# First block of a two-block transformer kernel: input projections on split halves with the low halves made by GpSimd, convolution sums in PSUM, decay logs moved ahead of the convolution's norm

## What is computed

```
h = rms_norm(x);  u = h @ w_in                      # 1024 x 6560
conv, c_q, c_kv, k_rope, hq, hf, hi, hg, u_gate = split(u)
y_a = silu(layer_norm(depthwise_conv31(a * sigmoid(g)) + b)) @ w_conv_out
y_b = attention(rms_norm(c_q) @ w_uq, rms_norm(c_kv) @ w_ukv, k_rope) @ w_attn_out
y_c = hgrn2(hq, hf, hi, hg) @ w_hgrn_out            # recurrence over time with decays
x = x + (sum over branches of sigmoid(u_gate_b) * y_b) @ w_out
x = x + relu(rms_norm(x) @ w_ff1)^2 @ w_ff2
```

## Time and profile before

| | |
|---|---|
| median of three runs | 2350.22 us (2348.99 to 2354.43) |
| the profiled execution, its own time | 2351.7 us |
| its span in the trace | 2349.8 us |
| mean granted TensorE clock | 0.97 of full speed |
| TensorE busy, share of the span | 95% |
| VectorE, ScalarE, GpSimd busy | 63%, 46%, 10% |
| first layer's input stage begins at | 21.0 us |
| second layer's input stage begins at | 609.4 us |

### The profile page before, as it was taken

How to read it: one execution, slowest core, us unless ns; L and a number is a source line. 1 busy time by engine, 2 the same in 40 slices (tenths; PEclk the granted TensorE clock), 3 DMA queues, 4 the chain that set the end, 5 groups by cost and what they waited for, 6 DMA issues and landing times.

```text
span 2349.8 us, 36652 instructions
## 1 busy us (share of the span) xinstructions
PE 2226.4 (95%) x13894; PEld 1878.1 (80%) x13894; DVE 1484.8 (63%) x2286; ACT 1085.5 (46%) x1525; POOL 239.9 (10%) x241
## 2 busy tenths in 40 slices
PE   8999999999999999899999789999999988999997
PEld 6878667999787866799976579887888577888786
DVE  2946355755394635575535577888775357788876
ACT  1142452444114244244433355676654355666665
POOL 1914000101091400011100000000000000000000
PEclk9999899999999989999999889999999998999999
DMA  4432123555343211456533236888865514688884
GB/s 164 144 117 82 63 63 126 175 185 171 125 143 117 81 65 64 144 175 199 185 133 97 74 118 216 306 297 309 296 214 162 161 55 153 227 311 304 304 295 145
DMA packets 109951, 397.38 MB, mean 169 GB/s; under 512 B 12104, under 2 KB 14160, under 8 KB 109520
## 3 DMA queue, kind: packets, MB, share of 16 engines
q1 hardware_dynamic: 108720, 393.98, 49.4%
q10 hardware_dynamic: 1056, 1.06, 0.1%
HBM read 393.93 MB, written 1.06 MB: 168 GB/s over the span
## 4 chain that ended last, share of the span: by engine, by line
PE 81%; DVE 12%; ACT 4%; issue 2%; DMA 1%; SPq 0%; DVEq 0%; ACTq 0%
PE psum L544 79%; DVE W_LO L1689 3%; PE psum L552 1%; DVE region L1694 1%; DMA ring<-in_weights 1%; DVE region L1697 1%; DVE RS L1726 1%; ACT region L1244 1%; ACT W_HI L1239 1%; DVE SQ L1694 1%; ACT SQ L1244 1%; ACT region L1248 0%; DMA PAR<-in_params 0%; ACT L1244 0%; DVE X_LO L1694 0%
## 5 line engine op out<-in xcount | busy, mean ns | idle before, releaser
L1689 DVE TENSOR_TENSOR W_LO<-ring,W_HI 128x1024 fp32r<-128x1024 f32 x435 | 533.0, 1225 | 223.9 <-ACT W_HI L1239 213.7
L1239 ACT ACTIVATE W_HI<-ring 128x1024 fp32r<-128x1024 f32 x435 | 461.8, 1062 | 323.7 <-PE psum L544 240.6
L544 PE MATMUL psum<-HN,ring 128*128 128x272 f32 (+1 forms) x1728 | 416.3, 402 | 9.8 <-DVE HN L1701 9.8
L544 PEld LDWEIGHTS psum<-HN,ring 128*128 128x128 f32 x1728 | 335.6, 196 | 83.1 <-issue 16.7
L544 PE MATMUL psum<-X_HI,W_HI 128*128 128x256 f32 x808 | 231.3, 286 | 8.9 <-DVE W_LO L1689 6.5
L544 PE MATMUL psum<-X_LO,W_HI 128*128 128x256 f32 x808 | 226.9, 281 | 0.0
L544 PE MATMUL psum<-X_HI,W_LO 128*128 128x256 f32 x808 | 226.7, 281 | 0.0
L1248 ACT ACTIVATE region<-psum 128x272 f32<-128x272 f32 (+10 forms) x223 | 89.0, 399 | 278.0 <-PE psum L544 255.6
L1689 DVE TENSOR_TENSOR W_LO<-SQ,W_HI 128x1024 fp32r<-128x1024 f32 x128 | 156.9, 1225 | 36.8 <-ACT W_HI L1239 32.9
L544 PE MATMUL psum<-W_HI,XG_HI 128*128 128x512 f32 x384 | 153.0, 398 | 17.3 <-DVE W_LO L1689 15.3
L544 PE MATMUL psum<-FN_HI,W_HI 128*128 128x272 f32 (+1 forms) x592 | 168.6, 285 | 0.0
(11 more groups left out here) (327 smaller groups left out, 4136.2 us busy)
## 6 DMA issues: line engine op xcount, KB each, us to landing
ring<-in_weights SPq DMA_DIRECT2D x616, 512.0 KB, 4.2
SQ<-in_weights SPq DMA_DIRECT2D x128, 512.0 KB, 4.8
XT<-in_x SPq DMA_DIRECT2D x1, 1088.0 KB, 5.0
CST<-in_consts SPq DMA_DIRECT2D x1, 1082.5 KB, 7.3
SQ<-bias_by_distance ACTq DMA_DIRECT2D x1, 1024.0 KB, 5.3
out<-XT SPq DMA_DIRECT2D x8, 128.0 KB, 1.9
PAR<-in_params SPq DMA_DIRECT2D x1, 572.0 KB, 8.3
bias_by_distance<-MIX ACTq DMA_DIRECT2D x1, 12.0 KB
```

The source lines that it names most:

```text
L544: ins = nc.tensor.matmul(dst, w, x, start=start, stop=stop, skip_group_check=True)
L1239: lane(nc.scalar.activation(W_HI[:, s % SPLIT, :], ring_slot(n), ACT.Copy), split_hi)
L1689: lane(nc.vector.tensor_tensor(W_LO[:, s % SPLIT, :], ring_slot(n), W_HI[:, s % SPLIT, :].bitcast(F32), ALU.subtract), split_lo)
```

## The change

1. The normed input of each layer is also kept as `HN_HI` (ScalarE copies, after the norm) and `HN_LO` (VectorE subtractions). All input chunks but the first two of a layer (`conv_a` 0 and `conv_g` 0) and all 24 gate chunks of a layer become split chunks: 50 in each layer. ScalarE makes their `W_HI`. GpSimd, not VectorE, makes their `W_LO`; it follows only after steps.
2. All four tiles of the convolution are made by VectorE. The running sum lies in PSUM bank 7, held for it; the gated inputs (`glu`) are made between the taps. GpSimd has no taps any more.
3. `hgrn_prep` is taken apart into `hgrn_scaled`, `hgrn_log`, `hgrn_sum` and `hgrn_strip`; the logs now stand ahead of `conv_norm`. ScalarE's Silu of the convolution and its first gate move behind them, and ScalarE's waits get further calls of `follow`. The root of the convolution's variance goes to a tile of its own.
4. The table `bucket` is loaded by a DMA of its own into a buffer used later, which frees room. `mla_q` lets go of its last chunk at its end.

The diff, cut to its core:

```diff
             def conv_in(l):
-                for j in range(4):
-                    project(("conv_a", l, j), hn, ready=None if j else till("normed", KT * 2 * l))
-                    project(("conv_g", l, j), hn)
+                banks.hold(("conv_sum", l), 7)
+                project(("conv_a", l, 0), hn, ready=till("normed", KT * 2 * l))
+                project(("conv_g", l, 0), hn)
+                for j in range(1, 4):
+                    project(("conv_a", l, j), hn_parts, ready=till("hn_split", KT * l) if j == 1 else None, by_pool=True)
+                    project(("conv_g", l, j), hn_parts, by_pool=True)
 ...
             def gate(l, b, m):
                 at = first_column(l)
-                project(("gate", l, b, m), lambda k: HN[:, k, at:], T - at)
+                project(("gate", l, b, m), lambda k: (HN_HI[:, k, at:], HN_LO[k][:, at:]), T - at, by_pool=True)
 ...
+                if r % 2 == 0:
+                    for k in range(KT):
+                        act.wait_ge(sem("normed"), KT * r + k + 1)
+                        fn(HN_HI[:, k, :], HN[:, k, :], ACT.Copy, sem("hn_high"))
 ...
+                else:
+                    for k in range(KT):
+                        dve.wait_ge(sem("hn_high"), KT * (r // 2) + k + 1)
+                        tt(HN_LO[k], HN[:, k, :], HN_HI[:, k, :].bitcast(F32), ALU.subtract, sem("hn_split"))
 ...
+                def taps(j, lo=0, hi=CONV_K):
+                    for i in range(lo, hi):
                         x, w, b = tap(l, j, i)
                         if i == 0:
-                            ts(CO[:, j, :], x, w, b, ALU.mult, ALU.add)
+                            ts(total, x, w, b, ALU.mult, ALU.add)
+                        elif i < CONV_K - 1:
+                            stt(total, x, w, total, ALU.mult, ALU.add)
                         else:
+                            stt(CO[:, j, :], x, w, total, ALU.mult, ALU.add, sem(f"conv_out{j}"))
+                half = CONV_K // 2 + 1
+                glu(0)
+                taps(0, 0, half)
+                glu(1)
+                taps(0, half)
+                glu(2)
+                taps(1, 0, half)
+                glu(3)
+                taps(1, half)
+                taps(2)
+                taps(3)
 ...
+            # on GpSimd
+            def split(s, n):
+                if not splits.by_pool[s]:
+                    return
+                pool.wait_ge(split_hi, s + 1)
+                lane(nc.gpsimd.tensor_tensor(W_LO[:, s % SPLIT, :], ring_slot(n), W_HI[:, s % SPLIT, :].bitcast(F32), ALU.subtract), split_pool)
+            follow = Follower(splits, split)
 ...
             for name, *args in SCHEDULE:
                 if name in steps:
                     steps[name](*args)
+                follow(("step", name, *args))
 ...
-        s += [("conv_in", l), ("conv_taps", l), ("hgrn_in", l), ("mla_in", l), ("hgrn_rows", l), ("conv_norm", l)]
-        s += [("gate", l, 0, 0), ("conv_var", l), ("mla_norm", l), ("hgrn_prep", l)]
+        s += [("conv_in", l), ("conv_taps", l), ("hgrn_in", l), ("mla_in", l), ("hgrn_scaled", l), ("hgrn_rows", l), ("hgrn_log", l)]
+        s += [("conv_norm", l), ("hgrn_sum", l), ("mla_norm", l), ("gate", l, 0, 0), ("conv_var", l), ("hgrn_strip", l), ("conv_silu", l), ("first_gate", l)]
```

More of the change, by code:

```diff
@@ L318, in __init__, with hold @@
         self.psum, self.full, self.free = psum, full, free
-        self.next, self.uses, self.of = 0, [0] * 8, {}
+        self.next, self.uses, self.of, self.held = 0, [0] * 8, {}, set()
+    def hold(self, key, bank):
+        self.of[key] = (bank, self.uses[bank])
+        self.uses[bank] += 1
+        self.held.add(bank)
     def take(self, pe, key, bank=None):
+        while bank is None and self.next in self.held:
+            self.next = (self.next + 1) % 8
         if bank is None:
@@ L462, in build_program @@
         HAT = at_region(3, 4, TP)
+        CONV_ROOT = HAT[:, 0, 0, :T]
+        with ExitStack() as first:
+            sb("unused_first", 4 * KT * T, stack=first)
+            HN_HI, low = (sb(f"HN_{p}", k, T, dtype=F32R, stack=first) for p, k in (("HI", KT), ("LO", KT - 1)))
+            assert (2 * KT - 1) * T <= 16 * 256
+            assert used[0] + T <= size
+            sb("unused_behind", 16 * 256 - (2 * KT - 1) * T + used[0], stack=first)
+            BUCKET = GATES[0][:, 0:2, :].rearrange("p a b -> p (a b)")[:, :384]
+            HN_LO = [low[:, k, :] for k in range(KT - 1)] + [sb("HN_LAST", T, dtype=F32R, stack=first)[:, :]]
         used[0] = work
@@ L558, in columns, with chunk @@
                 return tuple(p[:, lo : lo + n] for p in w) if isinstance(w, tuple) else w[:, lo : lo + n]
-            def chunk(split=False, routed=None):
+            def chunk(split=False, routed=None, by_pool=False):
                 n = state["n"]
@@ L623, in _ @@
             hn = lambda k: HN[:, k, :]
+            hn_parts = lambda k: (HN_HI[:, k, :], HN_LO[k])
             def start():
                 dst, done = take("bucket_bias")
-                mm(dst[:HEADS, :384], PAR[:BUCKETS, PARAMS["rel"][0] : PARAMS["rel"][0] + HEADS], cst("bucket", rows=BUCKETS), done=done)
+                mm(dst[:HEADS, :384], PAR[:BUCKETS, PARAMS["rel"][0] : PARAMS["rel"][0] + HEADS], BUCKET[:BUCKETS, :], done=done)
                 for l in range(DEPTH):
@@ L1338, in conv_norm, with conv_var, conv_silu, ahead @@
                 fn(SQ[:, : 4 * T], CO[:, :, :].rearrange("p k t -> p (k t)"), ACT.Square, sem("conv_squares"))
-                root(("conv_var", l), RS[:, :T], T, 512)
+            def conv_var(l):
+                root(("conv_var", l), CONV_ROOT, T, 512)
+            def conv_silu(l):
+                def ahead(m):
+                    wait_bank("gate", l, 0, m)
+                    follow(("gate", l, 0, m))
+                for m in range(3):
+                    ahead(m)
                 act.wait_ge(sem("conv_scaled"), l + 1)
@@ L1780, in norm, with conv_taps, glu @@
                         split_tile(FN_HI[r // 2][:, k, :], FN_LO[r // 2][:, k, :], HN[:, k, at:], sem("norm_split"))
+                else:
+                    for k in range(KT):
+                        dve.wait_ge(sem("hn_high"), KT * (r // 2) + k + 1)
+                        tt(HN_LO[k], HN[:, k, :], HN_HI[:, k, :].bitcast(F32), ALU.subtract, sem("hn_split"))
                 if r == 2:
                     zeros()
-            def conv_in(l):
-                for j in range(4):
+            def conv_taps(l):
+                bank, uses = banks.of["conv_sum", l]
+                dve.wait_ge(banks.free[bank], uses) if uses else None
+                nc.vector.memset(SM[:, 31:32], 0.0).then_inc(banks.full[bank], 1)
+                dve.wait_ge(banks.full[bank], uses + 1)
+                total = banks.tile(("conv_sum", l))[:, :T]
+                def glu(j):
                     src = wait_bank("conv_a", l, j)
```

93 lines of the change are left out of this document (52 added, 41 removed).

## The result

The changed kernel took **2397.65 us** (median of four runs, 2389.08 to 2400.66) against 2352.32 for the kernel before on the same chip. The ratio is 1.019, with an interval of 1.016 to 1.022: it is slower. I had forecast slower, but 2362 us and at most 2394; the loss is four times what I summed up. Its profiled execution took 2400.66 us (span 2398.9), 49.0 us over that of before.

A forecast was written before the change was run, and what follows sets the result against it. TensorE, busy 95% of the span, was taken to bound the kernel. Terms of +11.7 us in the first layer and -0.6 in the second added +11 to 2351.7, forecasting 2362 us, own range 2339 to 2377, wider range 2326 to 2394.

The forecast's parts named there:

- input stage: Input chunks: split chunks save 18.2 us a layer; the first layer gives back a 5.9 us stand and 2.1 of clock.
- first gates: Eight gates before `branch_out`: split chunks save 5.6 and 5.3 us, less 3 us given back for one late split.
- `branch_out` to first scores: Before the recurrence: GpSimd's splits delay `hgrn_args` 1, 22.7 us to first scores, plus a clock drop of 2.1.
- recurrence: Eight turns, each 2.3 us longer as GpSimd's differences wait behind splits, plus 4 us a layer for two clock drops.
- after it: Gates after the recurrence: split chunks save 5.6 and 5.3 us, less 1.5 for a root delayed by ScalarE's rounding.
- the first half of the pair: Recurrence, from ScalarE's read of gate 2 to turn 3, through rounding, split, differences, clamp and exponential: 12.5 us.
- The stand in the first layer's start: First layer's input stage: TensorE stands 5.9 us for the second `W_LO`, ready at 37.2, then a 2.1 us clock loss.
- 9.5 us a turn: Recurrence: a chain from gate i's end to gate i+2's end, for i = 2, takes 19.0 us for two turns.
- The price of a split: GpSimd's `W_LO` instruction: 1.95 us taken from its 128x1024 differences; the range keeps 2.89, a documentation estimate gave 2.25.
- The rival with the clock: Recurrence: the clock falls in each turn, +12 us in a layer rather than +4, total 2378; chance 0.07.
- stay ahead: Rival: GpSimd finishes splits early, so waits in the recurrence vanish and `branch_out` shrinks; about 2289 us; chance 0.14.
- Disturbed taps: Rival: PSUM sums don't part VectorE and GpSimd; taps 0.66, splits 2.9, `conv_mean` waits; about 2399 us; chance 0.13.

The follow-up runs named there:

- (2): Changed kernel with the eight gate chunks inside the recurrence of each layer plain again, as before the change: 2315.89 us, ratio 0.984.
- (1): Changed kernel with only GpSimd's list reordered, its differences for the next block ahead of its splits: 2338.31 us, ratio 0.991.
- (6): Kernel with plain gates in the recurrence, plus GpSimd's wait for the gate two turns earlier, without split work there: 2373.64 us, ratio 1.011.
- run 9: Changed kernel with useless float32 products on TensorE ahead of turns 1 to 6 (12, 6, 9, 12, 14, 12): 2386.08 us, ratio 1.016.
- run 10: Changed kernel with plain gates in the recurrence, four plain chunks at the first layer's start, and gate 6 ahead of the recurrence plain: 2297.30 us, ratio 0.977.
- experiment 4: Changed kernel with the convolution taps' running sum in SBUF instead of the held PSUM bank: 2481.94 us, ratio 1.053.
- (3): Changed kernel with eight useless float32 products on TensorE ahead of each of turns 1, 3 and 5: 2401.16 us, no change.

## Why the prediction failed, step by step

The second layer's rows are from the starts of its stages in both traces; all in microseconds against the kernel before:

| step | first layer: forecast, measured | second layer: forecast, measured |
|---|---|---|
| input stage | -10.2, -7.4 | -18.2, -16.8 |
| first gates | -2.6, -1.1 | -2.3, +0.6 |
| `branch_out` to first scores | +6.6, +5.6 | +3.2, +2.0 |
| recurrence | +22, +33.0 | +20.5, +32.7 |
| after it | -4.1, -2.4 | -3.8, -0.8 |

They make 45.4 us; 0.6 more is the later start of the first layer, and the remaining 3 us lie behind the second layer, in code that wasn't changed, and stay open.

**Right.** The direction, and the step where it is decided. GpSimd's list puts the split of gate i+3 ahead of the differences of block i+2, and this costs the recurrence: taking the splits out of there (2), or moving the differences ahead of them (1), wins 82 and some 60 us. The wait alone costs 48 us between the profiled executions and 58 in the medians (6). In the changed kernel the first half of the pair took 12.2 us (forecast 12.5). The stand in the first layer's start was 6.1 us (forecast 5.9), with a half clock from 39.9 to 45.7 behind it, but its size is in part luck: the low half was there at 39.8, not 37.2, since ScalarE rounded only after waiting 3.75 us for the store of the bias, and TensorE came to it at 33.9, not 31.3. The stands were 8.9 and 9.1 us ahead of the first scores (forecast 8). The taps were 0.506 us (0.50) and ended at 108.4 (105), 11 us ahead of their reader. The 22.7 us from `branch_out` to the scores were 23.8.

**Wrong: the term of the recurrence**, +22 where +33 was measured, and +20.5 where +32.7. Its 9.5 us a turn came from one pair of turns, i = 2, multiplied by eight; two drops of the clock stood beside it at 4 us. This went wrong:
- *The loop that I missed.* I let each chain pass through TensorE's gate. There is a shorter one, through ScalarE's list (exponential ahead of the gate's read), that closes within a turn and has a split in each, where my chain had one in two turns. It is in the rows of the changed kernel too: gate 3 was finished at 210.8 and read only at 214.06, right behind the exponential. In run 9 the clock is held up, and six turns of this loop take 61.6 us, 10.3 on the mean. With a split at my 1.95 and a clamp at 0.69 they would be 9.4 us each, so that my 9.5 was right for this loop too, by luck; what the miss did is that a dearer split counts in every turn. The stage has 86.1 us in run 9, +26 where I had +18. Some 2.5 of these 8 us are the filling's own: the scores of block 6 were copied out at 246.4, and the products held turn 6 until 248.9.
- *The price of a split.* In the six turns the splits took 2.34 to 2.74 us where I had 1.95, together 3.6 us more (2.44 is the mean of the whole changed kernel). I had taken the nearest row, GpSimd's differences. They have inputs that are repeated along an axis, and a split has two full ones; that this makes the difference wasn't tried. The Trainium skill, "GPSIMD Engine Reference", Elementwise — side-by-side cycle accounting, has 4497 ns for 2048 elements; the estimate of 2.25 us that I had set beside the sum is half of that. It is nearer, and still 8% low.
- *One clamp* took 2.48 us, beside GpSimd's differences of block 8: 1.8 us more, at nothing in my sum. The changed kernel has one of 2.47 at the same place.
- *The clock*, the largest part: +7 in a layer (run 9: 92.9 less 86.1), some +9 without the filling's delay, where I had +4. TensorE's own loss is larger, 4.4 us in the pair shown (10.5 for 6.0), but the loop through ScalarE hides part. The rival with the clock had the mechanism right; its +12 was too much, my +4 too little.

One slip in the range: it prices GpSimd's slower instructions at 0.94 us a turn and gives "two of each in a chain of two turns" as the reason, but the chain holds one of each. With a split and a difference in every turn, as the shorter loop has them, the same price would have been 1.9 us a turn.

**The rivals.** GpSimd did not stay ahead. With the order turned round (1) the kernel was still 49 us above that rival's 2289. Splits beside VectorE's products and clamps, which I had not priced, are a part of that; how large a part is open. It takes plain gates in the recurrence to come close to 2289 (2297.3, in run 10, with plain chunks at the start and gate 6 plain too). Disturbed taps are out by experiment 4.

**Smaller misses.** A split chunk of the input stage takes 3.02 us where I had 2.96, some 1.5 us in a stage. The first gates gave nothing in the second layer: one split there was 3.8 us late where I had given back 3 us, and the clock was at 0.75 and 0.68 in the 6 us behind it, which I had at nothing. In run 10 that wait is gone.

## What to carry to other kernels

When a helper job follows another engine's progress, draw the loop that it closes through every engine's list, not only through the busiest engine, and count the time of each by turn: here a loop that closes within one turn holds a split in each, the one that closes in two turns only one in both. Such work pays where nothing else stands behind it in its engine's list, as in the input stage, and costs many times its own length where something does: leaving out 16 splits of 100 here turned a loss of 2% into a gain of 1.6%. And a chain whose pieces grow from turn to turn is summed at its mean turn, with TensorE at the clock that its stands leave it.

## What the runs showed of the hardware

- Where VectorE works on two SBUF tensors beside steady GpSimd splits, its tap of 272 columns takes 0.926 us, with the sum in PSUM 0.506 (4 and the changed kernel). GpSimd hardly feels it: its split takes 2.47 and 2.44 us.
- A clamp with one SBUF input (1024 elements) takes 0.69 us alone and 2.87 when a GpSimd split of 2.35 starts with it (1).
- After a stand of 5.8 us TensorE does nearly a whole turn, block and gate at half clock, 10.5 us for 6.0. Where the stands were filled with work of no use (9) the clock stayed at 1.00 from 201 to 258 us. Smaller fillings that left 2 to 3 us idle (3) didn't hold it.
